# Gate and up products of the second block with the input's two parts side by side

## The chip, the cores and the metric

The kernel runs on one core of one Trainium2 chip. The metric is the device time of one execution in microseconds (us). All inputs lie in HBM when it begins, and the output is written there.

## The reference, cut to what matters

One sequence of 256 tokens with 1024 features goes through a first block (three mixers and a feed-forward stage) and then twice through a second block. Each pass of the second block has two feed-forward stages, with a width of 2816:

```python
def _swiglu(h, w_gu, w_down):
    gate, up = jnp.split(h @ w_gu, 2, axis=-1)
    return (jax.nn.silu(gate) * up) @ w_down

def second_block(x, w_in, ..., ffn_w_gu, ffn_w_down, ln_g, ln_b):
    alpha = (2 * DEPTH_2) ** 0.25
    for l in range(DEPTH_2):
        x = _layer_norm(alpha * x + 0.5 * _swiglu(x, ffn_w_gu[l, 0], ffn_w_down[l, 0]), ln_g[l, 0], ln_b[l, 0])
        mix = _token_mixers(x, w_in[l], ..., w_out[l], l)
        x = _layer_norm(alpha * x + mix, ln_g[l, 1], ln_b[l, 1])
        x = _layer_norm(alpha * x + 0.5 * _swiglu(x, ffn_w_gu[l, 1], ffn_w_down[l, 1]), ln_g[l, 2], ln_b[l, 2])
    return x
```

All of it is in float32. With `DEPTH_2` = 2 there are four such feed-forward stages. They are the place of the change.

## The kernel before, in words

The program is five written-out instruction streams, one for each engine (`tensor_program`, `scalar_program`, `vector_program`, `pool_program`, `sync_program`). Every engine runs its stream strictly in the written order. Named semaphores hold an engine until another has finished something. No planner and no pool decides anything: where an instruction stands in its stream is where the loops put it.

**Two parts of each number.** A product of float32 matrices is made of three products of a rounded type (fp32r). Each operand is split into a high part (a rounding copy) and a low part (operand less high part). `mm3` (lines 796 to 799) issues high by high, high by low and low by high into one accumulator. Since weights are the stationary operand in the stages of the change, it loads the same high weights twice. The input, transposed to features by tokens, stands in two tensors, `xTh` and `xTl`, each 128 x 8 x 256: eight groups k of 128 features, 256 tokens.

**A feed-forward stage.** Stage f = 0 belongs to the first block, f = 1 to 4 to the second. The width is cut into tiles of 128 features, 22 of them for f > 0. A tile j has one chunk of gate and up weights (128 x 2048) and one of down weights (128 x 1024). Its work is this.

- SyncE loads the chunks into staging buffers `st_gu` and `st_dn`.
- ScalarE rounds them to `hi_gu` (line 1306) and `hi_dn` (line 1313). VectorE subtracts to `lo_gu` (line 1636) and `lo_dn` (line 1641).
- TensorE makes `gate_up` (line 856): 8 k by 3 matmuls of 256 columns for gate, into half of a PSUM bank, and as many for up, into half of another bank. Two banks serve each in turn.
- ScalarE makes Silu of the gate from PSUM into `nonlin` (line 1383). VectorE multiplies it by up from PSUM and by 0.5 into `act32` (line 1789, the product). ScalarE rounds the product to `actTh` (line 1385). VectorE subtracts to `actTl` (line 1792).
- TensorE makes `down` (line 893): for each half m of the tokens, 6 matmuls of 512 columns, added into four banks over all tiles.

**Order on TensorE.** `ffn` (line 908) makes tiles 0 and 1 by tokens (`gate_up_tokens`, another layout). It then takes eight pairs (2 and 3, 4 and 5, up to 16 and 17): gate and up of both, then down of both. The last four tiles, 18 to 21, are the tail: gate and up of all four, then down of the four for m = 0, then for m = 1. `gate_up` waits for the tile's low weights, `down` for the tile's `actTl` (signal `prod_low`) and its low down weights.

**Order on ScalarE and VectorE.** Both walk tile by tile. After tile j's product come its high part and low part, then the split of the gate and up weights of chunk j + 2, then in some tiles the split of two down chunks (after the second tile of a pair, and after tile 19 in the tail). Only then comes anything of tile j + 1. After tile 20 and tile 21 the chunks split are the first two of the following stage. After the last stage there is none.

After the stage, `norm` on VectorE adds the four banks to `x`, first those of m = 0, and normalizes. TensorE then transposes `x`.

Of the kernel before, what the change touches and what calls it, by code (L numbers as in the profile page):

```python
# [7 lines left out]
F32 = mybir.dt.float32  # L8
# [167 lines left out]
def program(nc, A, C, out):  # L176
    ctx = ExitStack()
    with ctx:
# [6 lines left out]
        def signal(name):  # L185
            signals.append(Signal(ctx.enter_context(nc.semaphore(name))))
            return signals[-1]
# [18 lines left out]

        t_done, tok_done = signal("feature_product_done"), signal("token_product_done")
        gate_done, up_done, down_done, sum_done = (signal(n) for n in ("gate_done", "up_done", "down_done", "ffn_sum_done"))
        conv_a, conv_v, nonlin_done, prod_done, prod_high, prod_low = (signal(n) for n in (
            "conv_begun", "conv_tap_done", "nonlin_done", "product_done", "product_high", "product_low"))  # L210

# [40 lines left out]
        st_dn = [sb(f"st_dn{i}", [P, D]) for i in range(2)]  # L252
        x = sb("x", [P, M, D])
        n = sb("n", [P, M, D])
        xTh = sb("xTh", [P, KD, S], F32R)
        xTl = sb("xTl", [P, KD, S], F32R)


        at_down = -(-nc.sbuf_base // 32) * 32
# [255 lines left out]
        def wait_used(eng, c):  # L515
# [4 lines left out]
                eng.wait_ge(t_done.sem, t_done[c, 1 if width_of(c) == WCOLS else 0])  # L520
            else:
                eng.wait_ge(tok_done.sem, tok_done[c, 1])

        def hT_pair(t_, j):
            return t_[:, 2 * j:2 * j + 2, :].rearrange("p a b -> p (a b)")

        def hT_quad(t_, m, q):

# [265 lines left out]
        def tensor_program(pe):  # L794
# [61 lines left out]
            def gate_up(f, j, event=None):  # L856
                g, c = tile_no(f, j), CHUNK_NO["ffn", f, j]
                gate, up = bank[4 + g % 2], bank[6 + g % 2]
                hv, lv = pair_view(high_of(c), c), pair_view(low_of(c), c)
                wait_low(pe, c)  # L860
                for w, b, done in ((0, gate, gate_done), (1, up, up_done)):
                    for k in range(KD):
                        if event is not None and w == 0:
                            wait_h(event, 0, k)
                            wait_h(event, 1, k)
                        i = mm3(b[:, 0:S], (hv[:, w, k, :], lv[:, w, k, :]), (xTh[:, k, :], xTl[:, k, :]), k == 0, k == KD - 1)
                    i.then_inc(done.sem, done.one(g))

            def turn_products(g):
# [428 lines left out]
        def scalar_program(act):  # L1298
# [22 lines left out]
            def first_norm():  # L1321
                for m in range(M):
                    act.wait_ge(var_done.sem, var_done[0, m])
                    act.activation(sd[:, m:m + 1], ms[:, m:m + 1], ACT.Sqrt).then_inc(dev_done.sem, dev_done.one((0, m)))
                    act.wait_ge(scale_done.sem, scale_done[0, m])
                    for q in ((0, 1) if m == 0 else (1,)):
                        qs_ = slice(q * HALF, (q + 1) * HALF)
                        act.activation(n[:, m, qs_], x[:, m, qs_], ACT.Copy, scale=rs[:, m:m + 1]).then_inc(normed_a.sem, normed_a.one((0, m, q)))
                for j in range(KD // 2):
                    hi = hT_pair(xTh, j)  # L1330
                    act.wait_ge(h_turned.sem, h_turned[0, j])
                    for z in range(2):
                        i = act.activation(hi[:, z * S:(z + 1) * S], bank[4 + j][:, z * S:(z + 1) * S], ACT.Copy, scale=col("norm_mix", 2 * j + z))
                    i.then_inc(h_high.sem, h_high.one((0, j)))

            def norm(i):
# [19 lines left out]
            def ffn(f):  # L1356
# [16 lines left out]
                for j in range(by_tokens, tiles):  # L1373
# [6 lines left out]
                        act.wait_ge(conv_v.sem, conv_v[g, 0])  # L1380
                        act.activation(nonlin[:, t, :], conv[:, t, :], ACT.Gelu_apprx_tanh).then_inc(nonlin_done.sem, nonlin_done.one(g))
                    else:
                        act.activation(nonlin[:, t, :], gate[:, 0:S], ACT.Silu).then_inc(nonlin_done.sem, nonlin_done.one(g))
                    act.wait_ge(prod_done.sem, prod_done[g])
                    act.activation(actTh[:, g % RING, :], act32[:, t, :], ACT.Copy).then_inc(prod_high.sem, prod_high.one(g))  # L1385
                    if CHUNK_NO["ffn", f, j] + 2 < len(CHUNKS):
# [242 lines left out]
        def vector_program(dve):  # L1629
# [14 lines left out]
            def own():  # L1644

                dve.wait_ge(own_v.sem, own_v.n)
# [80 lines left out]
            def first_norm():  # L1727
# [13 lines left out]
                dve.wait_ge(scale_done.sem, scale_done[0, 1])  # L1741
                dve.tensor_scalar(n[:, 1, 0:HALF], x[:, 1, 0:HALF], rs[:, 1:2], None, ALU.mult).then_inc(normed_v.sem, normed_v.one((0, 1, 0)))
                for j in range(KD // 2):
                    hi, lo = hT_pair(xTh, j), hT_pair(xTl, j)
                    dve.wait_ge(h_high.sem, h_high[0, j])
                    for z in range(2):
                        zs = slice(z * S, (z + 1) * S)
                        i = dve.scalar_tensor_tensor(out=lo[:, zs], in0=bank[4 + j][:, zs], scalar=col("norm_mix", 2 * j + z), in1=hi[:, zs].bitcast(F32),
                                                     op0=ALU.mult, op1=ALU.subtract)
                    i.then_inc(h_low.sem, h_low.one((0, j)))  # L1750

# [4 lines left out]
            def ffn(f):  # L1756
# [17 lines left out]
                for j in range(by_tokens, tiles):  # L1774
                    g = tile_no(f, j)
                    t, gate, up = g % 2, bank[4 + g % 2], bank[6 + g % 2]
                    if f == 0:
                        for tap in (1, 0):
# [4 lines left out]
                            else:  # L1783
                                dve.wait_ge(conv_v.sem, conv_v[g, 1])
                            dve.scalar_tensor_tensor(out=cs, in0=gate[:, 0:S - lag], scalar=parc[:, tap, j:j + 1], in1=cs,
                                                     op0=ALU.mult, op1=ALU.add).then_inc(conv_v.sem, conv_v.one((g, tap)))
                    dve.wait_ge(nonlin_done.sem, nonlin_done[g])
                    dve.wait_ge(up_done.sem, up_done[g])
                    dve.scalar_tensor_tensor(out=act32[:, t, :], in0=nonlin[:, t, :], scalar=1.0 if f == 0 else 0.5, in1=up[:, 0:S],  # L1789
                                             op0=ALU.mult, op1=ALU.mult).then_inc(prod_done.sem, prod_done.one(g))  # L1790
                    dve.wait_ge(prod_high.sem, prod_high[g])
                    dve.tensor_tensor(actTl[:, g % RING, :], act32[:, t, :], actTh[:, g % RING, :].bitcast(F32), ALU.subtract).then_inc(
# [405 lines left out]
```

## Time and profile before

| | us |
|---|---|
| median of 3 runs | 1498.18 |
| lowest and highest run | 1497.56, 1499.16 |
| the profiled execution's own time | 1497.95 |
| its span, first to last instruction | 1496.6 |
| TensorE matmul busy in the span | 1396.9 (93%) |
| VectorE busy | 852.2 (57%) |
| ScalarE busy | 660.0 (44%) |

Times are those of the core. The span is the profiled execution from its first instruction to its last. An engine is busy while an instruction of it runs. PE is TensorE, PEld its weight loads, DVE VectorE, ACT ScalarE, POOL GpSimd, SP SyncE. PEclk is the clock granted to TensorE as a share of 2.4 GHz. Matmuls overlap, so the recorded length of one is longer than the step from its start to the start of the next: that step is what it costs in a row of them.

### The profile page before, as it was taken

To read this page: it belongs to the slowest core of one execution; us is meant where nothing else is said; L and a number is where in the kernel's file an instruction comes from. 1 tells how busy PE (TensorE), PEld (TensorE's weight loads), DVE (VectorE), ACT (ScalarE), POOL (GpSimd) and SP (SyncE) were. 2 spreads that over 40 slices of the span, in tenths; PEclk is the share of its full clock that TensorE was granted. 3 is DMA by queue.
4 is the path that set the end of the run, shared out by engine and by line. 5 is a ranking of instruction groups with operands and counts; after the bars stand their busy time and mean duration, and the time that the engine had idled before them with its cause. 6 is when DMAs were issued, how large, how long until landed. Compare 5 with 4: busy or idle time off the path is not lost.

```text
span 1496.6 us, 23293 instructions
## 1 busy us (share of the span) xinstructions
PE 1396.9 (93%) x9838; PEld 1297.4 (87%) x9838; DVE 852.2 (57%) x1137; ACT 660.0 (44%) x940; POOL 102.1 (7%) x141
## 2 busy tenths in 40 slices
PE   4799889999899998998899999899998999899997
PEld 4688889999799997987889999899997988889997
DVE  4578656656645456546654546655456545654545
ACT  4546444445444442545253444443352445344432
POOL 1123100000000001500000000000001500000000
PEclk9888789999999998999899999999998999899999
DMA  5332356666475654330566557466653431466561
GB/s 165 113 113 91 121 152 200 201 183 204 130 233 169 186 180 120 113 113 29 146 187 202 175 179 215 148 190 187 203 151 91 138 101 49 123 207 190 178 195 58
DMA packets 301202, 229.36 MB, mean 153 GB/s; under 512 B 13084, under 2 KB 283819, under 8 KB 301099
## 3 DMA queue, kind: packets, MB, share of 16 engines
q1 hardware_dynamic: 301082, 227.88, 50.3%
q8 instruction: 78, 1.28, 0.4%
q14 instruction: 26, 0.21, 0.0%
q10 hardware_dynamic: 16, 0.00, 0.0%
HBM read 226.80 MB, written 1.05 MB: 152 GB/s over the span
## 4 chain that ended last, share of the span: by engine, by line
PE 84%; DVE 9%; ACT 4%; DMA 1%; issue 1%; SPq 0%; POOL 0%; ACTq 0%; DVEq 0%
PE bank L797 25%; PE bank L798 24%; PE bank L799 24%; DVE lo_gu L1636 3%; PE bank L1212 2%; PE bank L1182 2%; PE bank L999 2%; ACT hi_gu L1306 2%; PE bank L1192 1%; DVE n L1686 1%; DVE stats L1663 1%; PE bank L807 1%; PE bank L1009 1%; DMA st_gu<-in_w_out 1%; DVE xTl L1651 1%
## 5 line engine op out<-in xcount | busy, mean ns | idle before, releaser
L797 PE MATMUL bank<-xTh,hi_gu 128*128 128x256 f32 x1864 | 533.2, 286 | 8.7 <-DVE big L1840 5.8
L798 PE MATMUL bank<-xTl,hi_gu 128*128 128x256 f32 x1864 | 531.2, 285 | 0.0
L799 PE MATMUL bank<-xTh,lo_gu 128*128 128x256 f32 x1864 | 531.1, 285 | 0.0
L1636 DVE TENSOR_TENSOR lo_gu<-st_gu,hi_gu 128x2048 fp32r<-128x2048 f32 (+2 forms) x146 | 324.1, 2223 | 170.0 <-ACT hi_gu L1306 170.0
L797 PEld LDWEIGHTS bank<-xTh,hi_gu 128*128 128x128 f32 x1864 | 361.8, 194 | 12.7 <-issue 8.1
L798 PEld LDWEIGHTS bank<-xTl,hi_gu 128*128 128x128 f32 x1864 | 361.8, 194 | 1.7
L799 PEld LDWEIGHTS bank<-xTh,lo_gu 128*128 128x128 f32 x1864 | 361.4, 194 | 0.0
L1306 ACT ACTIVATE hi_gu<-st_gu 128x2048 fp32r<-128x2048 f32 (+3 forms) x147 | 269.5, 1837 | 28.0 <-DMA st_gu<-in_ffn_w_val 10.7
L797 PE MATMUL bank<-hi_dn,actTh 128*128 128x512 f32 x436 | 171.7, 394 | 9.3 <-DVE actTl L1769 7.3
L798 PE MATMUL bank<-lo_dn,actTh 128*128 128x512 f32 x436 | 170.3, 391 | 0.0
L799 PE MATMUL bank<-hi_dn,actTl 128*128 128x512 f32 x436 | 169.8, 389 | 0.0
L1385 ACT ACTIVATE actTh<-act 128x256 fp32r<-128x256 f32 x101 | 42.2, 418 | 256.2 <-DVE act L1789 256.2
L1789 DVE SCALAR_TENSOR_TENSOR act<-nonlin,bank 128x256 f32<-128x256 f32 x101 | 42.5, 421 | 189.7 <-PE bank L799 183.4
L797 PE MATMUL bank<-hi_gu,xTh 128*128 128x256 f32 (+1 forms) x416 | 126.5, 304 | 9.9 <-DVE xTl L1651 9.0
L1641 DVE TENSOR_TENSOR lo_dn<-st_dn,hi_dn 128x1024 fp32r<-128x1024 f32 x109 | 129.0, 1219 | 6.5 <-ACT hi_dn L1313 6.0
L798 PE MATMUL bank<-lo_gu,xTh 128*128 128x256 f32 (+1 forms) x416 | 123.2, 296 | 0.0
L799 PE MATMUL bank<-hi_gu,xTl 128*128 128x256 f32 (+1 forms) x416 | 123.1, 296 | 0.0
L1313 ACT ACTIVATE hi_dn<-st_dn 128x1024 fp32r<-128x1024 f32 x109 | 109.5, 1046 | 16.5 <-DMA st_dn<-in_ffn_w_down 16.5
L797 PEld LDWEIGHTS bank<-hi_dn,actTh 128*128 128x128 f32 x436 | 82.0, 188 | 28.0 <-DVE actTl L1769 9.8
L797 PEld LDWEIGHTS bank<-hi_gu,xTh 128*128 128x128 f32 x416 | 86.0, 207 | 14.6 <-issue 12.7
L799 PEld LDWEIGHTS bank<-hi_dn,actTl 128*128 128x128 f32 x436 | 81.9, 188 | 17.5
L798 PEld LDWEIGHTS bank<-lo_dn,actTh 128*128 128x128 f32 x436 | 82.1, 188 | 15.0
(263 smaller groups left out, 1524.8 us busy)
## 6 DMA issues: line engine op xcount, KB each, us to landing
st_gu<-in_ffn_w_gu SPq DMA_DIRECT2D x176, 512.0 KB, 5.1
st_dn<-in_ffn_w_down SPq DMA_DIRECT2D x109, 512.0 KB, 6.4
st_gu<-in_w_in SPq DMA_DIRECT2D x23, 1024.0 KB, 5.4
st_gu<-in_w_out SPq DMA_DIRECT2D x12, 1024.0 KB, 5.2
st_gu<-in_ffn_w_gate SPq DMA_DIRECT2D x21, 512.0 KB, 5.1
st_gu<-in_ffn_w_val SPq DMA_DIRECT2D x21, 512.0 KB, 6.3
st_gu<-in_w_in SPq DMA_DIRECT2D x10, 512.0 KB, 4.1
gb<-in_ln_g SPq DMA_DIRECT2D x6, 512.0 KB, 6.6
```

What stands on the lines that cost most here:

```text
L797: pe.matmul(o, lhs[0], rhs[0], start=start, stop=False, **kw)
L798: pe.matmul(o, lhs[0], rhs[1], start=False, stop=False, **kw)
L799: return pe.matmul(o, lhs[1], rhs[0], start=False, stop=stop, **kw)
L999: i = pe.matmul(bank[bk][:, c0:c0 + P], kk[base:base + rws, blk, kt * P:(kt + 1) * P], qq[base:base + rws, blk, qt * P:(qt + 1) * P], star ...
L1182: t = pe.matmul(b[:, z * S:(z + 1) * S], q_, k_, start=not biased, stop=True, skip_group_check=biased)
L1212: t = pe.matmul(bank[4][:, z * HD:(z + 1) * HD], ptb[:, u % 2, (2 * z + kt) * P:(2 * z + kt + 1) * P], vb[:, kt, v0 + vh * HD:v0 + (vh + 1 ...
L1306: i = act.activation(high, staged, ACT.Copy)
L1313: act.activation(hi_dn[g % RING][:, :], st_dn[g % 2][:, :], ACT.Copy).then_inc(dn_high.sem, dn_high.one(g))
L1385: act.activation(actTh[:, g % RING, :], act32[:, t, :], ACT.Copy).then_inc(prod_high.sem, prod_high.one(g))
L1636: i = dve.tensor_tensor(low, staged, high.bitcast(F32), ALU.subtract)
L1641: dve.tensor_tensor(lo_dn[g % RING][:, :], st_dn[g % 2][:, :], hi_dn[g % RING][:, :].bitcast(F32), ALU.subtract).then_inc(dn_low.sem, dn_l ...
L1789: dve.scalar_tensor_tensor(out=act32[:, t, :], in0=nonlin[:, t, :], scalar=1.0 if f == 0 else 0.5, in1=up[:, 0:S], op0=ALU.mult, op1=ALU.m ...
```

## The change

The two parts of the input become one tensor, `xT`, 128 x 8 x 2 x 256: for each k the high part's 256 columns, then the low part's. `xTh` and `xTl` are now views of it. In the second block's tiles that `gate_up` makes (20 of the 22 in each of four stages), the high weights are multiplied by all 512 columns in one matmul, into a whole bank. Its left half then holds high by high, its right half high by low. The low weights by the high part go into the left half, as before. So each k takes two matmuls, of 512 and 256 columns, in place of three of 256.

Somebody has to add the halves. ScalarE copies the right half of the gate to `nonlin`, VectorE adds the left half, and ScalarE makes Silu of the sum. For up, ScalarE copies the right half to `act32`, and VectorE adds the left half. The product then reads SBUF only. The first block's stage and the tiles by tokens keep `mm3`. The diff (without the changes of the first norm, which write the same values to the new tensor):

```diff
+        gate_side, gate_summed, up_side = signal("gate_side_copied"), signal("gate_summed"), signal("up_side_copied")
...
-        xTh = sb("xTh", [P, KD, S], F32R)
-        xTl = sb("xTl", [P, KD, S], F32R)
+
+        xT = sb("xT", [P, KD, 2, S], F32R)
+        xTh, xTl = xT[:, :, 0, :], xT[:, :, 1, :]
...
-                        i = mm3(b[:, 0:S], (hv[:, w, k, :], lv[:, w, k, :]), (xTh[:, k, :], xTl[:, k, :]), k == 0, k == KD - 1)
+                        if f == 0:
+                            i = mm3(b[:, 0:S], (hv[:, w, k, :], lv[:, w, k, :]), (xTh[:, k, :], xTl[:, k, :]), k == 0, k == KD - 1)
+                        else:
+
+                            pe.matmul(b[:, :], hv[:, w, k, :], xT[:, k, :, :].rearrange("p a b -> p (a b)"), start=k == 0, stop=k == KD - 1,
+                                      skip_group_check=True)
+                            i = pe.matmul(b[:, 0:S], lv[:, w, k, :], xTh[:, k, :], start=False, stop=k == KD - 1, skip_group_check=True)
                     i.then_inc(done.sem, done.one(g))
...
-                        act.activation(nonlin[:, t, :], gate[:, 0:S], ACT.Silu).then_inc(nonlin_done.sem, nonlin_done.one(g))
+                        act.activation(nonlin[:, t, :], gate[:, S:2 * S], ACT.Copy).then_inc(gate_side.sem, gate_side.one(g))
+                        act.wait_ge(gate_summed.sem, gate_summed[g])
+                        act.activation(nonlin[:, t, :], nonlin[:, t, :], ACT.Silu).then_inc(nonlin_done.sem, nonlin_done.one(g))
+                        act.wait_ge(up_done.sem, up_done[g])
+                        act.activation(act32[:, t, :], bank[6 + g % 2][:, S:2 * S], ACT.Copy).then_inc(up_side.sem, up_side.one(g))
                     act.wait_ge(prod_done.sem, prod_done[g])
...
+                    else:
+                        dve.wait_ge(gate_side.sem, gate_side[g])
+                        dve.tensor_tensor(nonlin[:, t, :], nonlin[:, t, :], gate[:, 0:S], ALU.add).then_inc(gate_summed.sem, gate_summed.one(g))
+                    factor = up[:, 0:S]
+                    dve.wait_ge(up_done.sem, up_done[g])
+                    if f > 0:
+                        factor = act32[:, t, :]
+                        dve.wait_ge(up_side.sem, up_side[g])
+                        dve.tensor_tensor(factor, factor, up[:, 0:S], ALU.add).then_inc(own_v.sem, own_v.one())
+                        own()
                     dve.wait_ge(nonlin_done.sem, nonlin_done[g])
-                    dve.wait_ge(up_done.sem, up_done[g])
-                    dve.scalar_tensor_tensor(out=act32[:, t, :], in0=nonlin[:, t, :], scalar=1.0 if f == 0 else 0.5, in1=up[:, 0:S],
+                    dve.scalar_tensor_tensor(out=act32[:, t, :], in0=nonlin[:, t, :], scalar=1.0 if f == 0 else 0.5, in1=factor,
                                              op0=ALU.mult, op1=ALU.mult).then_inc(prod_done.sem, prod_done.one(g))
```

The order on VectorE, in stage 1, from the split of the weights after one pair's first tile to the second tile's low part. Before (bank6 holds the second tile's up):

```order
L1636 TENSOR_TENSOR lo_gu1<-st_gu1,hi_gu1 128x2048 [waits weights_high]
L1789 SCALAR_TENSOR_TENSOR act32<-nonlin,bank6 128x256 [waits up_done,nonlin_done]
L1792 TENSOR_TENSOR actTl<-act32,actTh 128x256 [waits product_high]
L1636 TENSOR_TENSOR lo_gu0<-st_gu0,hi_gu0 128x2048 [waits weights_high]
L1641 TENSOR_TENSOR lo_dn1_56<-st_dn1,hi_dn1_52 128x1024 [waits down_high]
```

So VectorE's part of the second tile begins with the product. The same place on VectorE in the changed kernel (bank4 holds the second tile's gate):

```order
L1644 TENSOR_TENSOR lo_gu1<-st_gu1,hi_gu1 128x2048 [waits weights_high]
L1796 TENSOR_TENSOR nonlin<-nonlin,bank4 128x256 [waits gate_side_copied]
L1802 TENSOR_TENSOR act32<-act32,bank6 128x256 [waits up_side_copied,up_done]
L1805 SCALAR_TENSOR_TENSOR act32<-nonlin,act32 128x256 [waits nonlin_done,vector_own]
L1808 TENSOR_TENSOR actTl<-act32,actTh 128x256 [waits product_high]
L1644 TENSOR_TENSOR lo_gu0<-st_gu0,hi_gu0 128x2048 [waits weights_high]
```

The addition for the gate stands behind the split of 2048 columns. Before, nothing of the second tile's gate was VectorE's, and ScalarE could make Silu while VectorE was splitting.

The order on ScalarE at the same place, first before:

```order
L1306 ACTIVATE hi_gu1<-st_gu1 128x2048 [waits up_done,weights_loaded1]
L1383 ACTIVATE nonlin<-bank4 128x256 [waits gate_done]
L1385 ACTIVATE actTh<-act32 128x256 [waits product_done]
L1306 ACTIVATE hi_gu0<-st_gu0 128x2048 [waits up_done,weights_loaded0]
L1313 ACTIVATE hi_dn1_52<-st_dn1 128x1024 [waits down_done,down_loaded1]
```

Silu reads PSUM and waits for TensorE alone. ScalarE in the changed kernel:

```order
L1311 ACTIVATE hi_gu1<-st_gu1 128x2048 [waits up_done,weights_loaded1]
L1387 ACTIVATE nonlin<-bank4 128x256 [waits gate_done]
L1389 ACTIVATE nonlin<-nonlin 128x256 [waits gate_summed]
L1391 ACTIVATE act32<-bank6 128x256 [waits up_done]
L1393 ACTIVATE actTh<-act32 128x256 [waits product_done]
L1311 ACTIVATE hi_gu0<-st_gu0 128x2048 [waits up_done,weights_loaded0]
```

One activation has become three, and the third (the copy of up's right half) stands behind Silu, which waits for VectorE's addition.

## Rows read from the trace of the kernel before

**Rows 1.** The page: the chain that ended last, its share of the span by engine.

```profile
PE 84%; DVE 9%; ACT 4%; DMA 1%; issue 1%; SPq 0%; POOL 0%; ACTq 0%; DVEq 0%
```

**Rows 2.** Windows (core, us, busy by engine, then PEclk): a short gap, stage 1, a long gap.

```profile
390.00:394.00 4.00, 2.93 (x26) 2.72 (x25) 1.66 (x4) 2.18 (x4) 0.00 (x0) 1.00 0.00 2
400.00:582.00 182.00, 179.79 (x1256) 168.32 (x1257) 99.66 (x105) 78.89 (x90) 0.93 (x1) 1.00 0.61 187
684.00:688.00 4.00, 1.42 (x7) 1.42 (x7) 1.89 (x3) 3.92 (x11) 0.00 (x0) 0.60 0.00 0
```

**Rows 3.** Timeline of DVE (start, length, line, idle before): two pairs of tiles.

```profile
447.43 0.42 DVE L1789 SCALAR_TENSOR_TENSOR act<-nonlin,bank 128x256 f32<-128x256 f32 x1 [3.94 <-PE bank L799]
450.13 2.29 DVE L1636 TENSOR_TENSOR lo_gu<-st_gu,hi_gu 128x2048 fp32r<-128x2048 f32 x1 [1.38 <-ACT hi_gu L1306]
453.19 0.42 DVE L1789 SCALAR_TENSOR_TENSOR act<-nonlin,bank 128x256 f32<-128x256 f32 x1 [0.76 <-PE bank L799]
454.10 0.43 DVE L1792 TENSOR_TENSOR actTl<-act,actTh 128x256 fp32r<-128x256 f32 x1 [0.48 <-ACT actTh L1385]
455.90 2.29 DVE L1636 TENSOR_TENSOR lo_gu<-st_gu,hi_gu 128x2048 fp32r<-128x2048 f32 x1 [1.38 <-ACT hi_gu L1306]
458.12 2.35 DVE L1641 TENSOR_TENSOR lo_dn<-st_dn,hi_dn 128x1024 fp32r<-128x1024 f32 x2
464.41 0.42 DVE L1789 SCALAR_TENSOR_TENSOR act<-nonlin,bank 128x256 f32<-128x256 f32 x1 [3.94 <-PE bank L799]
```

**Rows 4.** Timeline of ACT in the first of these pairs.

```profile
444.48 0.38 ACT L1383 ACTIVATE nonlin<-bank 128x256 f32<-128x256 f32 x1 [3.69 <-PE bank L799]
447.88 0.42 ACT L1385 ACTIVATE actTh<-act 128x256 fp32r<-128x256 f32 x1 [3.02 <-DVE act L1789]
448.21 1.90 ACT L1306 ACTIVATE hi_gu<-st_gu 128x2048 fp32r<-128x2048 f32 x1
```

**Rows 5.** Timeline of PE: last of gate, last of up, first of down (twice), next pair.

```profile
444.16 0.28 PE L799 MATMUL bank<-xTh,lo_gu 128*128 128x256 f32 x1
...
447.04 0.28 PE L799 MATMUL bank<-xTh,lo_gu 128*128 128x256 f32 x1
...
452.92 0.40 PE L797 MATMUL bank<-hi_dn,actTh 128*128 128x512 f32 x1
...
455.67 0.39 PE L797 MATMUL bank<-hi_dn,actTh 128*128 128x512 f32 x1
...
458.39 0.28 PE L797 MATMUL bank<-xTh,hi_gu 128*128 128x256 f32 x1
```

**Rows 6.** Lines by form: operations nearest to the added ones (busy, mean ns).

```profile
L1457 ACT ACTIVATE proj<-bank 128x256 f32<-128x256 f32 x8 | 3.0, 374 | 7.1 <-PE bank L799 7.1
L1381 ACT ACTIVATE nonlin<-conv 128x256 f32<-128x256 f32 x21 | 8.8, 418 | 43.5 <-DVE conv L1785 43.5
L1962 DVE TENSOR_TENSOR xTl<-bank,xTh 128x256 fp32r<-128x256 f32 x4 | 1.7, 425 | 1.2 <-ACT xTh L1517 1.2
```

**Rows 7.** Timeline: DVE before a dependent operation of its own, and that operation.

```profile
704.39 0.42 DVE L2066 TENSOR_TENSOR big<-gbo 128x256 f32<-128x256 f32 x1
704.85 0.42 DVE L2068 TENSOR_REDUCE big<-big 128x4 f32<-128x256 f32 x1
```

**Rows 8.** Timeline of DVE and PE: down waits for a tile by tokens.

```profile
400.11 0.42 DVE L1769 TENSOR_TENSOR actTl<-bank,actTh 128x256 fp32r<-128x256 f32 x1
400.59 0.50 PE L797 MATMUL bank<-hi_dn,actTh 128*128 128x512 f32 x1 [1.10 <-DVE actTl L1769]
400.93 0.39 PE L798 MATMUL bank<-lo_dn,actTh 128*128 128x512 f32 x1
```

**Rows 9.** Timeline of DVE: last split and norm behind stage 1; norm behind stage 2.

```profile
569.23 1.49 DVE L1636 TENSOR_TENSOR lo_gu<-st_gu,hi_gu 128x1280 fp32r<-128x1280 f32 x1 [0.74 <-ACT hi_gu L1306]
571.99 1.28 DVE L1657 SCALAR_TENSOR_TENSOR x<-x,bank 128x512 f32<-128x512 f32 x2 [1.26 <-PE bank L799]
...
929.98 1.28 DVE L1657 SCALAR_TENSOR_TENSOR x<-x,bank 128x512 f32<-128x512 f32 x2
```

More of the change, by code:

```diff
@@ L522, in wait_used @@
                 eng.wait_ge(tok_done.sem, tok_done[c, 1])
-        def hT_pair(t_, j):
-            return t_[:, 2 * j:2 * j + 2, :].rearrange("p a b -> p (a b)")
         def hT_quad(t_, m, q):
@@ L1329, in first_norm @@
                 for j in range(KD // 2):
-                    hi = hT_pair(xTh, j)
                     act.wait_ge(h_turned.sem, h_turned[0, j])
                     for z in range(2):
-                        i = act.activation(hi[:, z * S:(z + 1) * S], bank[4 + j][:, z * S:(z + 1) * S], ACT.Copy, scale=col("norm_mix", 2 * j + z))
+                        i = act.activation(xTh[:, 2 * j + z, :], bank[4 + j][:, z * S:(z + 1) * S], ACT.Copy, scale=col("norm_mix", 2 * j + z))
                     i.then_inc(h_high.sem, h_high.one((0, j)))
@@ L1743, in first_norm @@
                 for j in range(KD // 2):
-                    hi, lo = hT_pair(xTh, j), hT_pair(xTl, j)
                     dve.wait_ge(h_high.sem, h_high[0, j])
@@ L1747, in first_norm @@
                         zs = slice(z * S, (z + 1) * S)
-                        i = dve.scalar_tensor_tensor(out=lo[:, zs], in0=bank[4 + j][:, zs], scalar=col("norm_mix", 2 * j + z), in1=hi[:, zs].bitcast(F32),
+                        i = dve.scalar_tensor_tensor(out=xTl[:, 2 * j + z, :], in0=bank[4 + j][:, zs], scalar=col("norm_mix", 2 * j + z), in1=xTh[:, 2 * j + z, :].bitcast(F32),
                                                      op0=ALU.mult, op1=ALU.subtract)
```

## The prediction

> **What bounds the kernel now.** The chain that ended last comes first: 84% of it is PE [rows 1]. The second view is the windows. In stage 1 the matmuls cover 179.79 of 182 us at PEclk 1.00, which is 2.4 GHz, while DVE is busy 99.66 and ACT 78.89 [rows 2]. That says who is full, not how much room the others leave, and the change adds work to both. So the timelines come last. DVE's shows a pair of tiles from product to product, 464.41 - 447.43 = 16.98 us [rows 3]. PE's shows what fills it [rows 5]. From the last matmul of the first tile's up (447.04) to the first of down (452.92) there are 49 steps, 0.120 us each. From the second tile's down (455.67) to the next pair (458.39) there are 12 steps of 512 columns, 0.2267 each. The sum 96 x 0.120 + 24 x 0.2267 = 16.96 leaves nothing idle. PE bounds the pair.
>
> The room is in two places. The second tile's product begins at 453.19 and its low part ends at 454.10 + 0.43 = 454.53 [rows 3]; PE wants it at 455.67 [rows 5]. The spare time is 1.1 us. And the split for chunk j + 2 ends at 450.13 + 2.29 = 452.42, which is 5.38 us behind the last matmul of tile j's up. Inside a pair nobody wants it then. In the tail, gate and up of tile j + 2 begin 5.88 us behind that matmul, so the spare time there is 0.5 us.
>
> **What it removes.** In 4 stages x 20 tiles x 16 = 1280 places, matmuls of 256, 256 and 256 columns become 512 and 256. By the rows 3 x 0.120 = 0.360 becomes 0.2267 + 0.120 = 0.3467. A tile takes 16 x 0.3467 = 5.55 us in place of 5.76. The gain, if all of it counted, is 1280 x 0.0133 = 17.1 us. The trace has no 512 beside a 256 on the same accumulator, so I bound this step from both sides: 17.1 us or nothing. I take the first, since both widths cost their columns at 2.4 GHz plus the same 13 ns.
>
> The Trainium skill (TensorE: Matmul & The Clock Gate, on the extra 2.5 ns between matmuls) says that a warm matmul costs its columns over 2.4 GHz plus about 2.5 ns. The trace has 13.3 ns over the columns at either width, with a weight load before each. By the page an estimate of the gain would be 1280 x 2.5 ns = 3.2 us in place of 17.1.
>
> **What it adds.** Each of 80 tiles gets two ACT copies of 128x256 from PSUM (0.374 by the nearest row, 0.38 in Silu's), a Silu that reads SBUF (0.418 as Gelu's, in place of 0.38), and two DVE additions with one operand in PSUM (0.425) [rows 4, 6]. As busy time that is 63 us on ACT and 68 on DVE. Neither becomes full, and if it only lay beside PE it would cost nothing. It doesn't. The additions stand in the chain from up to down, and the gate's also stands behind the 2.29 us split. Nothing else covers it.
>
> **The second tile of a pair**, counted from the start of the last matmul of the first tile's up (zero). Handoffs are as the rows show: PE to ACT 0.32 from a matmul's start (444.16 to 444.48), DVE to ACT and back 0.03 (447.85 to 447.88), ACT back to back 0.09 of overlap (448.30 to 448.21), DVE about the same (458.19 to 458.12, 0.07) [rows 3 to 5]. DVE behind its own result costs 0.04 (704.81 to 704.85) [rows 7].
>
> - first tile: copy of up ends at 0.69, sum 1.14, product 1.60, high part 2.05
> - split of the next chunk: ACT ends at 3.86, DVE at 6.17
> - second tile: gate sum ends at 6.50, Silu 6.95, copy of up 7.24, sum of up 7.69, product 8.15, high 8.60, low 9.05
> - PE starts 0.06 later (400.53 to 400.59) [rows 8]: 9.11; and its first step after such a wait is 0.34 in place of 0.23 [rows 8], so 9.22 counts
>
> PE is there at 0.12 + 5.55 + 2.72 (first down) = 8.39. It waits 0.83 us. The new period is 9.22 + 2.72 + 5.55 - 0.12 = 17.37, against 16.98. The two tiles' gain of 0.43 is more than given back: +0.39 us per pair. By 8 pairs and 4 stages that is +12.5 us.
>
> **The tail** (four gate-ups in a row), same count from tile 18. Tile 20's low weights are ready at 6.17, and with 0.06 and 0.07 for the restart PE begins at 6.30 where 5.67 was due: 0.63. Tile 19's high part ends at 8.60, ACT's split for 21 at 10.41, DVE's at 12.72, PE begins at 12.85 where 11.85 was due: 1.00. Then ACT and DVE split two down chunks (DVE until 14.98), and behind that come tile 20's sums and product (16.96), its split for the next stage (21.53), tile 21's sums, product and low part (24.42). PE wants that at 18.40 + 3 x 1.36 = 22.48 and gets it at 24.59: 2.11. In all 3.74 less four tiles' gain of 0.85 is +2.89 in stages 1 to 3. Stage 4 has no next chunk and loses 1.63 - 0.85 = 0.78. Sum +9.4 us.
>
> **The norm behind.** After stage 1, DVE was idle 1.26 us before the norm's first addition [rows 9]. Now its last split ends at 26.64, where PE's sum is ready at 25.95 + 0.2: +0.5, and the same in stage 3. After stage 2 both last splits have 2048 columns, DVE went from split to norm without idle time [rows 9], and the split now ends at 28.08: +1.9. PE's transposes wait for this norm, so it counts. Sum +2.8 or so.
>
> 12.5 + 9.4 + 2.8 = 24.7. The profiled execution took 1497.95 us, 0.23 under the median of 1498.18, and its span 1496.6. So 1498.2 + 24.7 = 1522.9. The steps of the norm are the least sure (it may be half of that), so I say 1522.
>
> **Bounds of that case.** If a copy takes 0.36, no restart cost follows, and ACT's and DVE's back-to-back steps overlap by 0.1 everywhere, the chain is 0.3 shorter: some 40 places (32 pairs, tails, norms) give back 12 us, hence 1510. If every handoff among the four new ones costs 0.05 more, 40 x 0.2 = 8 us, hence 1530.
>
> **Rivals.**
>
> *Hidden after all: faster.* PE's own gain is the whole story if the low part of the second tile comes before PE has done the first down. The place is the wait of PE before the second down, the price 0.83 us per pair. For it: DVE is busy 55% and ACT 43% of stage 1 [rows 2], and today's spare time is 1.1 us. Against it: the chain of 14 steps is each from a row, and it needs 9.22 where 8.39 are there. The point from which it decides: with a chain shorter by 24.7 / 40 = 0.6 us the kernel is where it was. With 0.83 the pairs gain 32 x 0.43 = 13.7 us, the tails still lose about 5, and the time is 1489.
>
> *No gain in the matmuls.* The 512 and 256 take the 0.360 us of the three. Then waits shrink, but the pair is longer: period 9.22 + 2.72 + 5.76 - 0.12 = 17.58, another +0.21, or 6.8 us in 32 pairs, and about 1 in the tails: 1530. For it: nobody has seen the mix. Against it: equal 13 ns at both widths. The rule of 2.5 ns gives nearly this, with a gain of 0.2 us out of 1.
>
> *The clock falls in the new waits.* In the gap around 684 us the clock was 0.60 over 4 us, PE busy 1.42 of them [rows 2]; at 392, with a wait of 1.07 us, it stayed 1.00. At 0.60 a stretch of 4 us does the work of 2.4, and if the next 4 are alike the price of one fall is 3 us. The 0.8 us waits are shorter than the harmless one; those of 2.1 in three tails lie between. If all three fall, +9: 1532.
>
> **How the numbers follow.** Forecast 1522 (own range 1510 to 1530): 0.70. No gain in the matmuls (1530): 0.09. Clock (1532): 0.09. A shorter chain that ends within 0.2%, 3 us, of before (about what a measurement of this kernel tells from no change): 0.05. Hidden, faster (1489): 0.07. So faster 0.07, same 0.05, slower 0.88. The range 1508 to 1536 leaves out the last two cases and little of the others on either side.
>
> **What would show it.** In the changed profile the matmul group of 512 columns has 1280 members and the step to the next 256 is 0.227. PE waits before down for VectorE's low part some 32 times by 0.7 to 0.9 us, and pairs of tiles are 17.3 to 17.5 apart. Three waits stand in each tail, the last about 2 us. PEclk stays 1.00. If instead pairs are 16.6 apart with no wait before down, the chain was counted too long and the first rival holds; if pairs are 17.6 apart, the second.

## The result and the profile after

The changed kernel took 1533.73 us (median of 4 runs, 1532.23 to 1545.69); the kernel before took 1497.87 us beside it (4 runs, 1493.87 to 1499.16). The ratio is 1.0249, with a 95% interval of 1.0195 to 1.0304. Run again without an edit it gave 1534.3 us and a ratio of 1.0259 (1.0233 to 1.0285). I had forecast 1522 with a range of 1508 to 1536: slower, and by the right mechanism, but by 24 us where it was 36. The range for that mechanism alone was 1510 to 1530, and 1533.73 lies above it.

The page of the changed kernel says first who holds whom. It answers to [rows 1]:

```profile
span 1531.0 us, 21133 instructions
PE 56%; DVE 25%; ACT 14%; issue 3%; DMA 1%; SPq 0%; DVEq 0%; ACTq 0%
```

TensorE's share of the chain that ended last fell from 84% to 56%. The difference is on VectorE and ScalarE. Yet neither became full: stage 1's windows are these (PE, PEld, DVE, ACT and POOL busy, then PEclk), against [rows 2].

```profile
400.00:582.00 182.00, 173.74 (x893) 144.17 (x893) 107.40 (x127) 88.19 (x124) 0.00 (x0) 1.00 0.59 178
```

VectorE is at 59% and ScalarE at 48%. What they do is serial. The view of waits of the changed kernel names what TensorE waited for (total us, times, longest):

```profile
PE bank L796 <- DVE actTl L1808: 27.0, 37, 2.4
PE bank L869 <- DVE lo_gu L1644: 4.6, 8, 0.8
```

The 37 waits of down for a low part are one in each of the 32 pairs, three long ones in the tails of stages 1 to 3, and two of the first block's stage, which the kernel before has too. The 8 waits of gate-up are two in each of four tails. These are the places that the forecast named.

VectorE's timeline of one pair in the changed kernel answers to [rows 3] (start, length, line, idle before):

```profile
465.62 0.42 DVE L1802 TENSOR_TENSOR act<-act,bank 128x256 f32<-128x256 f32 x1 [2.48 <-ACT act L1391]
466.07 0.42 DVE L1805 SCALAR_TENSOR_TENSOR act<-nonlin,act 128x256 f32<-128x256 f32 x1
466.98 0.42 DVE L1808 TENSOR_TENSOR actTl<-act,actTh 128x256 fp32r<-128x256 f32 x1 [0.48 <-ACT actTh L1393]
468.79 2.29 DVE L1644 TENSOR_TENSOR lo_gu<-st_gu,hi_gu 128x2048 fp32r<-128x2048 f32 x1 [1.39 <-ACT hi_gu L1311]
471.00 0.41 DVE L1796 TENSOR_TENSOR nonlin<-nonlin,bank 128x256 f32<-128x256 f32 x1
472.24 0.42 DVE L1802 TENSOR_TENSOR act<-act,bank 128x256 f32<-128x256 f32 x1 [0.82 <-ACT act L1391]
472.69 0.42 DVE L1805 SCALAR_TENSOR_TENSOR act<-nonlin,act 128x256 f32<-128x256 f32 x1
473.60 0.42 DVE L1808 TENSOR_TENSOR actTl<-act,actTh 128x256 fp32r<-128x256 f32 x1 [0.48 <-ACT actTh L1393]
```

The gate's sum (L1796) has no idle time before it: it starts the moment the split ends. From the first tile's sum of up to the second tile's low part it takes 474.02 - 465.62 = 8.40 us. ScalarE at the same place, against [rows 4]:

```profile
465.13 0.38 ACT L1391 ACTIVATE act<-bank 128x256 f32<-128x256 f32 x1 [1.54 <-PE bank L871]
466.53 0.42 ACT L1393 ACTIVATE actTh<-act 128x256 fp32r<-128x256 f32 x1 [1.02 <-DVE act L1805]
466.85 1.90 ACT L1311 ACTIVATE hi_gu<-st_gu 128x2048 fp32r<-128x2048 f32 x1
468.66 0.36 ACT L1387 ACTIVATE nonlin<-bank 128x256 f32<-128x256 f32 x1
471.44 0.42 ACT L1389 ACTIVATE nonlin<-nonlin 128x256 f32<-128x256 f32 x1 [2.43 <-DVE nonlin L1796]
471.77 0.37 ACT L1391 ACTIVATE act<-bank 128x256 f32<-128x256 f32 x1
```

The copy of up ends at 465.51, the sum starts at 465.62: 0.11 us by these rounded rows, and 0.10 before rounding in each of the 80 tiles. The high part ends at 466.95 and the low part starts at 466.98: 0.03. One handoff costs three times the other. TensorE, against [rows 5]:

```profile
456.44 0.50 PE L796 MATMUL bank<-hi_dn,actTh 128*128 128x512 f32 x1 [0.56 <-DVE actTl L1808]
456.77 0.40 PE L797 MATMUL bank<-lo_dn,actTh 128*128 128x512 f32 x1
...
459.29 0.39 PE L869 MATMUL bank<-xT,hi_gu 128*128 128x512 f32 x1
...
459.98 0.40 PE L869 MATMUL bank<-xT,hi_gu 128*128 128x512 f32 x1
460.22 0.28 PE L871 MATMUL bank<-xT,lo_gu 128*128 128x256 f32 x1
460.34 0.40 PE L869 MATMUL bank<-xT,hi_gu 128*128 128x512 f32 x1
460.57 0.28 PE L871 MATMUL bank<-xT,lo_gu 128*128 128x256 f32 x1
460.69 0.40 PE L869 MATMUL bank<-xT,hi_gu 128*128 128x512 f32 x1
...
464.81 0.28 PE L871 MATMUL bank<-xT,lo_gu 128*128 128x256 f32 x1
```

A wide and a narrow step of TensorE together take 0.353 us on average (459.98 to 460.34, then to 460.69), not 0.347. The last row is the last of a first tile's up. The second tile's low part ends 9.21 us behind it (474.02), with TensorE due at 464.81 + 0.12 + 5.65 + 2.72 = 473.30. Read from the start of one pair's first gate-up to the next, the time has gone here, in us:

| part, four stages | before | after | more | forecast |
|---|---|---|---|---|
| 32 pairs | 16.98 each | 17.65 to 17.66 each | 21.6 | 12.5 |
| tails, first gate-up to last down starts | 33.71 each | 37.02, 37.03, 37.05, 34.90 | 11.2 | 9.4 |
| all else, norms among it | | | 1.6 | 2.8 |
| span | 1496.6 | 1531.0 | 34.4 | 24.7 |

### The profile page after: what moved, and what is told of

Its sections match the earlier page's. It is cut to its first block, busy times and chain, and to the rows that moved or that the text cites. A ratio compares the mean times of both kernels' runs of the same rounds, so it can differ in the third digit from the quotient of the medians.

```text
span 1531.0 us, 21133 instructions
## 1 busy us (share of the span) xinstructions
PE 1400.4 (91%) x8558; PEld 1224.1 (80%) x8558; DVE 916.2 (60%) x1297; ACT 714.9 (47%) x1100; POOL 102.1 (7%) x141
## 4 chain that ended last, share of the span: by engine, by line
PE 56%; DVE 25%; ACT 14%; issue 3%; DMA 1%; SPq 0%; DVEq 0%; ACTq 0%
PE bank L796 11%; PE bank L797 10%; PE bank L798 10%; DVE lo_gu L1644 10%; PE bank L869 9%; ACT hi_gu L1311 8%; PE bank L871 5%; DVE act L1805 2%; PE bank L1217 2%; DVE act L1802 2%; PE bank L1187 2%; ACT act L1391 2%; DVE n L1694 1%; ACT nonlin L1389 1%; PE bank L1004 1%
## 5 line engine op out<-in xcount | busy, mean ns | idle before, releaser
L869 PE MATMUL bank<-xT,hi_gu 128*128 128x512 f32 x1280 | 454.2, 399 | 4.6 <-DVE lo_gu L1644 4.6
L871 PE MATMUL bank<-xT,lo_gu 128*128 128x256 f32 x1280 | 359.2, 281 | 0.0
L869 PEld LDWEIGHTS bank<-xT,hi_gu 128*128 128x128 f32 x1280 | 240.5, 188 | 66.1 <-DVE lo_gu L1644 7.1
L1311 ACT ACTIVATE hi_gu<-st_gu 128x2048 fp32r<-128x2048 f32 (+3 forms) x147 | 269.5, 1837 | 31.5 <-DMA st_gu<-in_ffn_w_val 12.5
L871 PEld LDWEIGHTS bank<-xT,lo_gu 128*128 128x128 f32 x1280 | 241.7, 189 | 1.4
L796 PE MATMUL bank<-hi_dn,actTh 128*128 128x512 f32 x436 | 176.7, 405 | 34.4 <-DVE actTl L1808 27.0
L796 PE MATMUL bank<-xT,hi_gu 128*128 128x256 f32 x584 | 170.0, 291 | 8.6 <-DVE big L1856 5.8
L797 PE MATMUL bank<-xT,hi_gu 128*128 128x256 f32 x584 | 167.8, 287 | 0.0
L798 PE MATMUL bank<-xT,lo_gu 128*128 128x256 f32 x584 | 167.7, 287 | 0.0
L796 PE MATMUL bank<-hi_gu,xT 128*128 128x256 f32 (+1 forms) x416 | 127.5, 307 | 9.9 <-DVE xT L1659 8.9
L797 PE MATMUL bank<-lo_gu,xT 128*128 128x256 f32 (+1 forms) x416 | 124.2, 298 | 0.0
L798 PE MATMUL bank<-hi_gu,xT 128*128 128x256 f32 (+1 forms) x416 | 124.0, 298 | 0.0
L796 PEld LDWEIGHTS bank<-xT,hi_gu 128*128 128x128 f32 x584 | 114.8, 197 | 11.2 <-issue 7.8
L797 PEld LDWEIGHTS bank<-xT,hi_gu 128*128 128x128 f32 x584 | 114.9, 197 | 0.3
L798 PEld LDWEIGHTS bank<-xT,lo_gu 128*128 128x128 f32 x584 | 114.6, 196 | 0.0
L1802 DVE TENSOR_TENSOR act<-act,bank 128x256 f32<-128x256 f32 x80 | 33.7, 421 | 125.7 <-ACT act L1391 125.7
```

The source lines that it names most:

```text
L796: pe.matmul(o, lhs[0], rhs[0], start=start, stop=False, **kw)
L797: pe.matmul(o, lhs[0], rhs[1], start=False, stop=False, **kw)
L798: return pe.matmul(o, lhs[1], rhs[0], start=False, stop=stop, **kw)
L869: pe.matmul(b[:, :], hv[:, w, k, :], xT[:, k, :, :].rearrange("p a b -> p (a b)"), start=k == 0, stop=k == KD - 1, skip_group_check=True)
L871: i = pe.matmul(b[:, 0:S], lv[:, w, k, :], xTh[:, k, :], start=False, stop=k == KD - 1, skip_group_check=True)
L1311: i = act.activation(high, staged, ACT.Copy)
```

## The experiments

**The parts by themselves.** The first asks whether the wide matmul or the sums lose the time. `pe_alone` keeps TensorE's stream and takes the rest back:

```diff
-                        act.activation(nonlin[:, t, :], gate[:, S:2 * S], ACT.Copy).then_inc(gate_side.sem, gate_side.one(g))
-                        act.wait_ge(gate_summed.sem, gate_summed[g])
-                        act.activation(nonlin[:, t, :], nonlin[:, t, :], ACT.Silu).then_inc(nonlin_done.sem, nonlin_done.one(g))
...
+                        act.activation(nonlin[:, t, :], gate[:, 0:S], ACT.Silu).then_inc(nonlin_done.sem, nonlin_done.one(g))
```

> The wide matmul alone: TensorE as in the changed kernel, ScalarE and VectorE as before the change, reading the left half only (the product of high weights by low input is left out of the result). Theory A: nothing is late for TensorE any more; two steps take 0.353 in place of 0.360, so 1280 x 0.0067 = 8.6 us are gained on the kernel before: 1489 us, pairs 16.75 apart, no wait before down but in the tiles by tokens. Rival (the time is lost on TensorE, in the wide product or its clock): above 1498, most of the 34 us still there.

It took 1485.23 us against 1495.31: ratio 0.9933 (0.9913 to 0.9954). Pairs stand 16.794 us apart, and the view of waits has no wait for a low part beside the ten that the kernel before has:

```profile
PE bank L796 <- DVE actTl L1772: 7.3, 8, 1.1
PE bank L796 <- DVE actTl L1795: 2.3, 2, 1.3
```

So the wide matmul is a gain, 0.19 us per pair. Pairs had been expected 16.75 apart and a gain of 8.6 us. By the trace the pairs gained 6.0 and the tails 1.7 (33.28 each, where it was 33.71); the medians are 10 apart, and the rest lies in stretches that the two kernels have in common, of which more below. `side_alone` is the other half:

```diff
-                            pe.matmul(b[:, :], hv[:, w, k, :], xT[:, k, :, :].rearrange("p a b -> p (a b)"), start=k == 0, stop=k == KD - 1,
-                                      skip_group_check=True)
+                            pe.matmul(b[:, 0:S], hv[:, w, k, :], xTh[:, k, :], start=k == 0, stop=False, skip_group_check=True)
+                            pe.matmul(b[:, S:2 * S], hv[:, w, k, :], xTl[:, k, :], start=k == 0, stop=k == KD - 1, skip_group_check=True)
```

> The sums alone: high weights by low input go into the right half of the bank by a matmul of 256 columns of their own, three matmuls of 256 as before the change; ScalarE and VectorE add the halves as in the changed kernel. Theory A: the chain holds the pair, and one gate-up of 5.76 in place of 5.65 us is in the period: 17.76 us, so 32 x 0.11 = 3.4 us more than the changed kernel and up to 1 in the tails: 1536 us. Rival (the loss is in the wide matmul): 1498 to 1505.

1533.62 us, ratio 1.0278 (1.0231 to 1.0325), pairs 17.77 apart. (It leaves something out of the sums. The Trainium skill, PSUM — Partial Sum Buffer, The four PSUM rules, says that the first matmul of a group clears the has_written bits for the whole bank. Here the right half's first matmul stands behind the left's, so by that rule the left half lacks its first product; no trace shows these bits. The count, widths and order of the instructions are what the time is read from.) With narrow matmuls alone the whole loss is there. A pair is 0.11 longer than in the changed kernel, where the expectation had 0.11: one slower gate-up in a period that the chain sets. That is the sign that TensorE no longer bounds the whole pair: two gate-ups got slower by 0.11 each, and one of them shows.

> The changed kernel once more, unedited, to have its time beside the others on the same chip: 1532 to 1535 us by both theories, since its four runs gave 1532.23, 1532.33, 1535.13 and 1545.69. Pairs of tiles 17.65 us apart.

That was the control: 1534.3 us, pairs 17.661.

**The handoff of 0.10.** `one_wait` takes one of VectorE's two waits away. ScalarE's copy, for which the other waits, has itself waited for up.

```diff
-                    dve.wait_ge(up_done.sem, up_done[g])
-                    if f > 0:
+                    if f == 0:
+                        dve.wait_ge(up_done.sem, up_done[g])
+                    else:
                         factor = act32[:, t, :]
                         dve.wait_ge(up_side.sem, up_side[g])
```

> VectorE's own wait for up_done ahead of the sum of up is taken away for the second block; the wait for ScalarE's copy of up's right half stays, and that copy has waited for up_done itself. Theory A, chain of handoffs (the pair is set by the serial chain between ScalarE and VectorE, and the handoff to the sum of up costs 0.10 in place of 0.03 us because two waits stand before the instruction and the last one is the one that ends late): the handoff falls to 0.03, a pair is 0.14 shorter (17.51), 4.5 us in 32 pairs and about 1 in the tails: 1527 us. Rival B (0.10 is what a VectorE addition costs behind a copy that reads PSUM, whatever waits stand before it): no change, 1532 to 1534.

1523.97 us, ratio 1.0189 (1.0165 to 1.0213), pairs 17.50 apart (expected 17.51). The handoff went to 0.03 in all 80 tiles. In 32 pairs that is 5 us, and in the tails 1.1 (36.72 in three, 34.74 in the last); the medians are 10 apart. `waits_swapped` keeps both waits and turns their order:

```diff
-                    dve.wait_ge(up_done.sem, up_done[g])
                     if f > 0:
-                        factor = act32[:, t, :]
                         dve.wait_ge(up_side.sem, up_side[g])
+                    dve.wait_ge(up_done.sem, up_done[g])
+                    if f > 0:
+                        factor = act32[:, t, :]
```

> The changed kernel with VectorE's two waits ahead of the sum of up in the other order: first for ScalarE's copy (which ends late), then for up_done (long over). Theory A (the wait that stands last before the instruction costs 0.07 more when it is the one that ends late): handoff 0.03, pairs 17.50 us apart as in the kernel with one wait. Rival C (two waits before an instruction cost 0.07 in either order): handoff 0.10, pairs 17.65.

A single execution: 1524.29 us, span 1523.0, pairs 17.50 to 17.51 apart in all four stages. The sum of up in VectorE's timeline of that kernel, idle time before it 0.76 where it was 0.82:

```profile
470.84 0.42 DVE L1803 TENSOR_TENSOR act<-act,bank 128x256 f32<-128x256 f32 x1 [0.76 <-ACT act L1391]
```

So it isn't the number of waits. It is which one ends late: that which stands last before the instruction costs 0.07 us more. Rival C falls, and rival B too.

A second case lies in the kernels with narrow tails, below. There VectorE's product waits first for up, which ends late, and then for Silu; in the kernel before, the two stand the other way round. For tile 18 of stage 1, the last matmul of up and then the product, before:

```profile
548.92 0.28 PE L799 MATMUL bank<-xTh,lo_gu 128*128 128x256 f32 x1
549.31 0.42 DVE L1789 SCALAR_TENSOR_TENSOR act<-nonlin,bank 128x256 f32<-128x256 f32 x1 [3.94 <-PE bank L799]
```

and in `tail_narrow`:

```profile
555.63 0.28 PE L798 MATMUL bank<-xT,lo_gu 128*128 128x256 f32 x1
555.95 0.42 DVE L1807 SCALAR_TENSOR_TENSOR act<-nonlin,bank 128x256 f32<-128x256 f32 x1 [2.92 <-PE bank L798]
```

From start to start that is 0.39 us and 0.32, the same 0.07. It is 0.39 in 72 tiles of the kernel before and 0.32 in nine of `tail_narrow`: all those in which VectorE stood idle before the product.

**The split in the chain.** `reordered` builds on `one_wait` and moves VectorE's split behind the second tile:

```diff
+                    paired = f > 0 and j < tiles - TAIL
+                    if paired and j % 2 == 1:
+                        weights_low(CHUNK_NO["ffn", f, j] + 1)
-                    if CHUNK_NO["ffn", f, j] + 2 < len(CHUNKS):
+                    if CHUNK_NO["ffn", f, j] + 2 < len(CHUNKS) and not (paired and j % 2 == 0):
                         weights_low(CHUNK_NO["ffn", f, j] + 2)
```

> The changed kernel without VectorE's extra wait, and in the pairs VectorE makes the split of chunk j + 2 only behind the second tile's low part, in place of between the two tiles; ScalarE's order is kept. Theory A: the split of 2.29 us leaves the chain, the second tile's low part comes 8.2 us behind the last matmul of the first tile's up, where TensorE is at 8.5; no wait in the pairs, 16.8 us apart as in the run of the wide matmul alone, 32 x 0.7 = 22 us less than the run without the extra wait (1524): 1502 us. Rival B (ScalarE, which makes Silu, copies and splits in one row, holds the pair, not the split on VectorE): pairs stay above 17.3, over 1517 us.

1504.33 us, ratio 1.0053 (1.0033 to 1.0073), pairs 16.793 apart, as with the wide matmul alone. VectorE's timeline of a pair in it:

```profile
450.12 0.42 DVE L1796 TENSOR_TENSOR nonlin<-nonlin,bank 128x256 f32<-128x256 f32 x1 [1.65 <-ACT nonlin L1387]
452.33 0.42 DVE L1803 TENSOR_TENSOR act<-act,bank 128x256 f32<-128x256 f32 x1 [1.79 <-ACT act L1391]
452.79 0.42 DVE L1806 SCALAR_TENSOR_TENSOR act<-nonlin,act 128x256 f32<-128x256 f32 x1
453.69 0.42 DVE L1809 TENSOR_TENSOR actTl<-act,actTh 128x256 fp32r<-128x256 f32 x1 [0.48 <-ACT actTh L1393]
454.04 4.49 DVE L1644 TENSOR_TENSOR lo_gu<-st_gu,hi_gu 128x2048 fp32r<-128x2048 f32 x2
```

All additions are still there. With the splits behind them (4.49 us for two) they cost the pair nothing. Little is left: the first split ends at 454.04 + 2.29 = 456.33, and TensorE begins the next pair with it at 457.22.

**The tails.** `tail_narrow` is the changed kernel with tiles 18 to 21 as before the change, but for the order of the two waits ahead of the product. In `gate_up` the condition becomes this one, and ScalarE and VectorE branch in the same way:

```diff
-                        if f == 0:
+                        if f == 0 or j >= FFN_TILES[f] - TAIL:
```

> The changed kernel, but the last four tiles of each stage (18 to 21) as before the change: three matmuls of 256, Silu and the product from PSUM. Theory A: each tail takes 33.7 us again where it took 37.0 (34.9 in the last stage), in all 11 us, and the norms behind them wait 2 to 3 us less: 1520 us; pairs stay 17.65 apart. Rival B (the tails lose only by the same handoffs as the pairs, about 0.2 us a tile): 1530 us.

1514.13 us, ratio 1.0129 (1.0102 to 1.0156). Tails take 33.71 again in all four stages, pairs 17.65. By the tails' own spans that is 11 us, as expected. From the last down of stage 2 to the next pair it takes 24.42 us, where the changed kernel took 27.65 and the kernel before 24.46, so another 3.2 goes there. The profiled spans, 1531.0 and 1519.8, are only 11 apart since the stretches ahead of the pairs of stage 1 and behind its tail, where no matmul or sum differs, took 3.7 us longer in the second trace. The medians of the runs are 20 apart. Part of that is the granted clock, below.

`pairs_only` joins `reordered` with that edit.

> The order of the previous kernel in the pairs, and the tails as before the change. Theory A: pairs 16.8 and tails 33.7 us, so the gain of 32 x 0.186 = 6 us is kept and nothing given back: 6 us below the kernel before on the same chip, 1489 us. Rival B (other losses remain, since the tiles wait elsewhere): 1495 or more.

1490.78 us over 10 runs beside 1496.23 for the kernel before, ratio 0.9974 (0.995 to 0.9997), pairs 16.793, tails 33.71. It's faster than the kernel before, barely.

**Alternating or grouped.** `pairs_grouped` issues the wide matmuls of a product first:

```diff
                         else:
                             pe.matmul(b[:, :], hv[:, w, k, :], xT[:, k, :, :].rearrange("p a b -> p (a b)"), start=k == 0, stop=k == KD - 1,
                                       skip_group_check=True)
-                            i = pe.matmul(b[:, 0:S], lv[:, w, k, :], xTh[:, k, :], start=False, stop=k == KD - 1, skip_group_check=True)
+                    if f > 0 and j < FFN_TILES[f] - TAIL:
+                        for k in range(KD):
+                            i = pe.matmul(b[:, 0:S], lv[:, w, k, :], xTh[:, k, :], start=False, stop=k == KD - 1, skip_group_check=True)
```

> The previous kernel with the eight wide matmuls of a product first and the eight narrow ones behind, in place of alternating. Theory A with a cost of alternating (0.235 us for a wide step between narrow ones, 0.227 among its like): a tile is 16 x 0.008 = 0.13 us shorter, 64 tiles give 8 us: 1481 us, pairs 16.53. Rival (a wide step costs 0.235 in this product wherever it stands, or the first steps behind any change are slow): pairs stay at 16.8, 1489 us.

1485.27 us over 10 runs, ratio 0.9925 (0.9885 to 0.9965), pairs 16.614: 0.18 less than alternating, where 0.26 was expected. Its TensorE timeline of one product and the next:

```profile
442.23 2.00 PE L868 MATMUL bank<-xT,hi_gu 128*128 128x512 f32 x8
444.07 1.12 PE L872 MATMUL bank<-xT,lo_gu 128*128 128x256 f32 x8
445.02 2.00 PE L868 MATMUL bank<-xT,hi_gu 128*128 128x512 f32 x8
```

Eight wide steps take 444.07 - 442.23 = 1.84, 0.230 each; eight narrow ones 0.95. The wide step is 0.235 among narrow ones, 0.230 in an eight, and 0.2267 late in a down of 24 ([rows 5]: 455.67 to 458.39). So alternating does cost something, though less than expected, and the rival (pairs stay at 16.8) is out. This is the best version here, 0.75% below the kernel before.

## Why the prediction was right, and short by ten microseconds

The ten are by spans, 34.4 where 24.7 was counted; by medians it was 36 against 24.

**Bound and mechanism.** That TensorE fills the pair, that the additions join the chain behind the split, and that two tiles' gain is more than given back: `pe_alone`, `side_alone` and `reordered` show each of these by itself. The count of waits (32, and three places in the tails) was as forecast. The rival "hidden after all" is out. Its argument, spare busy share, is just what misled: with VectorE at 59% TensorE stood idle 0.8 us a pair.

**Where it was luck.** My own range ended at 1530. That 1533.73 still lies in the range I gave is owed to the room added for two rivals, no gain in the matmuls (1530) and the clock (1532), and neither made the time: the first isn't so, and the second cost 1.5 us in the first trace. One sign that I had named even points the wrong way: pairs 17.6 apart were to mean no gain in the matmuls, and they are 17.655 apart. `pe_alone` settles it: a gain is there, 0.19 us a pair where 0.43 was counted. What brought the pairs to 17.655 is the following.

**The pair: 17.37 counted, 17.655 measured.** Three terms were too small.

- The handoff from ScalarE's copy to the sum of up, taken as 0.03, was 0.10, and stands twice in the chain: 0.15 of the 0.28. `one_wait` gives 17.50. Its like was in the rows shown: VectorE's product began 0.39 us behind the last matmul of up, Silu 0.32 behind that of gate [rows 3 to 5], and the product too had two waits, the late one last. I put the difference down to the engine, and the product in `tail_narrow` shows that it was the order of the waits.
- The step of the wide matmul, taken as 0.2267 from downs, was 0.235, so a tile takes 5.65 us in place of 5.55: 0.11. Of the stated gain of 0.0133 us per place about half is there. `pe_alone` keeps (16.98 - 16.794) x 32 = 6.0 us in the pairs, where 32 x 0.43 = 13.7 was counted.
- The first steps of down behind a wait are slower than the one restart step that I counted: 2.85 (456.44 to 459.29) where 2.83 was counted, 0.02.

Together 0.28 a pair, 9 us in 32. The span was 9.7 us short: the pairs 9.1 and the tails 1.8, less 1.2 in all else.

The rule of the Trainium skill weighed there (TensorE: Matmul & The Clock Gate, about 2.5 ns between matmuls) gave 3.2 us for the whole gain. By the pairs of `pe_alone` the saving is 0.186 / 32 = 0.006 us per place: between the page's 0.0025 and my 0.0133. Neither is right in this stream.

**The tails.** Forecast +2.89 and +0.78, measured +3.31 to +3.34 and +1.18: same mechanism, same two mis-sized terms. Without the late wait (`one_wait`) a tail is 0.3 us shorter, and one gate-up at 5.65 is 0.11. In `tail_narrow` the whole of it goes.

**The norms.** I had 0.5 us of delay behind stages 1 and 3 and 1.9 behind stage 2. TensorE's transposes start 0.50 and 0.48 us behind the last down in stages 1 and 3 of the changed kernel, where it was 0.24, and 1.95 behind it in stage 2, where it was 0.23. That is 0.26, 0.24 and 1.72: right in kind, a little less in size. The 3.2 us measured in stage 2 between the last down and the next pair has another part, the rival of the clock. The windows of the changed kernel there:

```profile
951.00:955.00 4.00, 2.10 (x12) 1.16 (x10) 3.85 (x8) 1.09 (x3) 0.00 (x0) 1.00 0.57 162
955.00:959.00 4.00, 3.49 (x17) 3.52 (x18) 3.93 (x9) 0.51 (x2) 0.00 (x0) 0.57 0.02 4
```

TensorE was idle for some 2.4 us of these eight, most of it ahead of the transposes, and PEclk is 0.57 in the second window, so nearly all of that window was at the lower level. Before the change it was 1.00 at this place. In `one_wait`, `waits_swapped` and `side_alone` it didn't fall there, and the stretch took 26.2 to 26.3 us in place of 27.65: the fall cost 1.4 to 1.5 us. In the unedited second run of the changed kernel it happened in the tails of stages 2 and 3 instead, behind the long wait. These are the windows of stage 2:

```profile
942.00:946.00 4.00, 2.08 (x9) 1.39 (x8) 2.23 (x5) 1.99 (x4) 0.00 (x0) 0.99 0.51 147
946.00:950.00 4.00, 4.00 (x12) 3.16 (x11) 3.04 (x3) 2.21 (x2) 0.00 (x0) 0.59 0.42 115
```

Those two tails took 38.6 us in place of 37.0. But behind stage 2 TensorE has to wait for VectorE's norm in any case. The transposes in the first trace of the changed kernel, then in the second:

```profile
953.35 1.32 PE L806 MATMUL bank<-ident,x 128*128 128x128 f32 x8 [1.56 <-DVE x L1701]
954.31 1.32 PE L806 MATMUL bank<-ident,x 128*128 128x128 f32 x8
```

The tail began at 914.37 in the first and at 915.33 in the second, so both start 38.98 us behind it: in stage 2 the fall in the tail cost nothing. In stage 3 the transposes came 38.85 us behind the tail's start where it was 37.53, so there it cost 1.3. The rival that I gave 9% is thus real, at nothing to 1.5 us a fall where I had 3, and comes and goes from run to run with the same program. It doesn't explain the shortfall: the first trace has no fall in any tail and one behind stage 2.

What I took from the rows, 1.07 us of idle time harmless and 2.1 on the border, is too simple. In the trace of `reordered` TensorE stood idle for 0.87 and 0.84 us between 380 and 383.3, each shorter than 1.07, and its clock fell behind them:

```profile
383.00:387.00 4.00, 3.77 (x19) 3.81 (x20) 3.52 (x10) 0.22 (x2) 0.00 (x0) 0.59 0.00 0
```

The granted clock also goes with the spread of the runs. Each has its span and its mean granted clock; these are four of the ten of `pairs_grouped`:

| span, us | mean clock |
|---|---|
| 1475.8 | 0.969 |
| 1482.4 | 0.962 |
| 1494.5 | 0.956 |
| 1498.8 | 0.953 |

From the first to the last the clock is 0.016 lower. If the whole span went by the clock, that would be 24 us of 1480, and the span is 23 longer. `tail_narrow` had its profiled run at 0.961 (1519.8) and its other three at 0.965 to 0.967 (1511.5 to 1513.5). So by my estimate a difference of medians of four runs carries up to 10 us of clock. The periods in the traces are the sharper measure: a kernel's means of the four stages agree to 0.01 us.

**What stays open.** Where the clock fell in the runs without a trace can't be said. The traces say where it differs between runs: the changed kernels have the same program until the pairs of stage 1, yet the first pair began at 401.83 us in `pe_alone` and at 408.79 in `tail_narrow`, with PEclk at 0.94 and 0.93 over the first 400. Why the last of two waits costs more when it is the late one isn't shown. Why a wide matmul costs 0.008 us more among narrow ones was not found either.

## What to carry to other kernels

Before work is added to engines at half load, count the serial chain that it joins, from the bound engine's last instruction to its next wait, with what stands ahead of it in each queue: here 8.5 us were there and 9.3 were needed, with VectorE 59% busy. If such work must be added, first move what isn't urgent behind it (here a split whose chunk TensorE wants 3 us after the place to which the split was moved). Then look at the order of waits before one instruction.

## What the runs showed of the hardware

- Two waits ahead of one VectorE instruction: 0.10 us from the end of ScalarE's instruction to the start of VectorE's when the late one stands last in the code (the changed kernel, 80 of 80), 0.03 when it stands first (`waits_swapped`, 80 of 80). Putting it first was worth as much as taking the other away, 0.15 us a pair. Behind TensorE it was the same 0.07: 0.39 and 0.32 from the start of the last matmul.
- A matmul of 512 columns started 0.235 us before its follower in a row that alternates with 256, 0.230 in rows of eight, 0.2267 late in a row of 24. The narrow ones took 0.118 to 0.120 in all three. The cause was not looked for.
- The first step of TensorE behind a wait was 0.33 to 0.34 us at the full clock, for matmuls of 512 columns in downs and in gate-ups alike, where a step in a row is 0.23.
- Behind an idle stretch of 1.8 to 1.9 us in a tail TensorE's clock fell to the lower level for some 3 us in two of three tails of one run (`again`, steps of 0.43 us in place of 0.23), and in none of the first run of the same program. It also fell behind two shorter ones, 0.87 and 0.84 (`reordered`, near 383).
- What a fall cost depended on what TensorE waited for next: nothing where the norm held it in any case, 1.3 to 1.5 us elsewhere. Granted clock and span of the runs go together as closely as above.
